# Two experts per gathered slot: value products on alternating 64-column halves of TensorE in a two-layer mixture kernel

## The chip, the cores and the metric

The kernel runs on one core of one Trainium2 chip. The metric is the device time in microseconds (us) of one execution. Each kernel is one launch. All data are float32. The core has TensorE (PE, whose weight loads are shown as PEld), VectorE (DVE), ScalarE (ACT), GpSimd (POOL) and SyncE (SP), and 16 DMA engines that bring data from the device memory (HBM) into on-chip memory (SBUF).

## The reference, cut to what matters

Two layers work on 256 latent tokens of 1024 channels (and in layer 0 also on 256 context tokens). Each layer mixes tokens and then applies an expert mixer, which takes most of the time:

```python
def peer(h, wq, subkeys, u_tab, v_tab):
    ...
    idx = i1 * PEER_KEYS + i2                 # 8 heads x 16 experts per token
    g = jax.nn.softmax(cv, axis=-1)
    ...
    def block(args):
        tb, ib, gb = args
        act = jax.nn.gelu(jnp.einsum('td,thkd->thk', tb, u_tab[ib]).astype(jnp.float32))
        return jnp.einsum('thk,thkd->td', (gb * act).astype(tb.dtype), v_tab[ib])
```

Each token picks 128 of 16384 experts. For each of them a row u (1024 numbers) is multiplied with the token's activations to one number, which goes through gelu and is weighted, and a row v (1024 numbers) is added to the token's output with that weight. The kernel does this for latent tokens of layer 0 (stage 0), context tokens of layer 0 (stage 1) and latent tokens of layer 1 (stage 2): 3 stages of two 128-token tiles with 128 experts each, 768 tile-experts of 1 MB, 805 MB in all.

## The kernel before

**The slot pipeline.** A slot `s` is one tile-expert: partition p of the ring buffer `uv` (RING = 8 places of 8 KB per partition) holds row u and row v of the expert that token p has in place `s % 128`. The work of a slot passes through all engines:

- POOL (`gathers`, L1050) waits until the ring place is free (`uv_used`) and issues an indirect DMA of 128 rows of 8 KB.
- DVE (`dot`, L1593) multiplies u with the token's activations `h2` and sums to `dots`.
- ACT (`weigh`, L1221, L1223, L1225) takes gelu, multiplies by the gate `gw`, and writes the diagonal matrix `diag` (128x128, weight of token p at row p, column p).
- PE (`add_values`, L983) multiplies `diag` (the stationary side) with v in two products of 512 columns and adds them up in PSUM, in `acc`. Each product in float32 is two MATMUL instructions in the profile. The last one frees the ring place.
- After the 128 slots of a tile DVE adds `acc`, times a gate, to `x` (`close`).

**The order of the work.** One list (`schedule`) is walked by PE, ACT and DVE. It has "slot" entries, "values" entries two slots later (LAG = 2), and between them "step" entries, which are all other work: projections (`query`, L786), scores (L957), searches for the best experts (`find`, six parts on DVE), the mixing of the next stage. `place` and `spread` fix the slot after which a step stands. Each engine works through its part strictly in order. Ahead of slot 0 (the opening, up to 176 us) and between the last slot of stage 1 and the first slot of stage 2 (the gap, about 1575 to 1664 us) only steps run, and there most ring places hold weight blocks. A gather into such a place waits until its block has been multiplied (`left`).

**What the change touches.** `turn_back` (L933) makes `h2`, token by token, out of `hT`, in which channels lie along the partitions: 8 transposes on PE and 2 evictions of 512 columns on ACT for each tile. It runs six times: for stage 0 tile 0 in the opening, stage 0 tile 1 soon after the first slots, twice among the slots for stage 1, for stage 2 tile 0 in the gap, and for stage 2 tile 1 some 60 us later. `find` part 5 (L1564, L1569) writes 16 expert numbers (`idx`) and 16 gates (`gw`) for each tile and head, 48 times in all.

## Time and profile before

| | before |
|---|---|
| median of 3 runs | 2360.29 us (2359.01 to 2362.58) |
| the profiled execution | span 2360.1 us, 0.2 us from the median |
| PE busy | 2079.7 us (88%) |
| DVE busy | 1609.6 us (68%) |
| POOL busy | 1019.5 us (43%) |
| ACT busy | 953.4 us (40%) |
| moved by DMA | 939.43 MB, 398 GB/s over the span |
| chain that ended last | PE 36%, DMA 33%, DVE 13% |

"Busy" of PE counts each matmul up to a modelled end, which overlaps the start of the next one, so it overstates how much of PE is used. "The chain that ended last" is followed backwards from the last instruction, each time to what released it. "GB/s" is what the 16 DMA engines moved in a stretch.

### The profile page before, as it was taken

What the parts mean: (1) busy time and instruction counts of PE and PEld (TensorE: products, weight loads), DVE (VectorE), ACT (ScalarE), POOL (GpSimd) and SP (SyncE); (2) the same over time, 40 slices, a digit from 0 to 9 for tenths busy, and PEclk for the clock granted to TensorE, in tenths of its full rate; (3) what the DMA queues carried; (4) which work ended last, traced back from release to release, by engine and by line L of the source; (5) the groups of instructions that cost most, each with busy time, mean ns of one, the idle gap of its engine ahead of it and who ended that gap; (6) DMA issues with size and microseconds to landing.
All of it is one profiled execution on the core that took longest, in us unless ns stands there. A gap on an engine that the chain in (4) does not pass through costs nothing.

```text
span 2360.1 us, 24134 instructions
## 1 busy us (share of the span) xinstructions
PE 2079.7 (88%) x6896; PEld 1123.8 (48%) x6896; DVE 1609.6 (68%) x3952; ACT 953.4 (40%) x2791; POOL 1019.5 (43%) x868
## 2 busy tenths in 40 slices
PE   8998998899998988988898998798899988777787
PEld 7775554455564434544454544346455533222222
DVE  3855668967766568788866677855765887666454
ACT  2014434543334444444454333534543444444333
POOL 0004444344334444444444454530333555566774
PEclk9999999999999999999999999999999999999999
DMA  9979999999999999999999999996799999999997
GB/s 400 375 291 382 395 399 421 407 421 421 421 420 421 415 421 404 421 421 417 391 421 421 421 421 421 416 370 254 284 365 379 415 421 421 422 421 421 422 421 318
DMA packets 132595, 939.43 MB, mean 398 GB/s; under 512 B 14720, under 2 KB 17920, under 8 KB 18944
## 3 DMA queue, kind: packets, MB, share of 16 engines
q0 software_dynamic: 110592, 805.36, 82.8%
q1 hardware_dynamic: 21888, 132.68, 13.8%
q8 instruction: 55, 0.90, 0.2%
q14 instruction: 60, 0.49, 0.1%
HBM read 936.93 MB, written 1.05 MB: 397 GB/s over the span
## 4 chain that ended last, share of the span: by engine, by line
PE 36%; DMA 33%; DVE 13%; issue 7%; POOL 6%; ACT 5%; POOLq 0%; SPq 0%; DVEq 0%; ACTq 0%
DMA uv<-uv_dram,stage_idx 31%; PE psum L983 19%; PE psum L786 9%; DVE uv L1593 6%; POOL uv L1050 5%; PE psum L768 4%; PE psum L926 1%; DMA uv<-in_dram 1%; ACT diag L1225 1%; DMA uv<-ada_dram 1%; ACT wv L1223 1%; DVE h L1282 1%; PE psum L704 1%; PE psum L957 1%; ACT gel L1221 1%
## 5 line engine op out<-in xcount | busy, mean ns | idle before, releaser
L983 PE MATMUL psum<-uv,diag 128*128 128x512 f32 x3072 | 1447.1, 611 | 227.8 <-ACT diag L1225 217.6
L1050 POOL DMA_INDIRECT uv<-uv_dram,stage_idx x768 | 985.9, 1284 | 1052.3 <-PE psum L983 829.5
L1593 DVE CUSTOM_DVE_ANT_0 uv<-uv,h 128x1024 f32<-128x1024 f32 x768 | 935.1, 1226 | 554.6 <-DMA uv<-uv_dram,stage_idx 545.2
L983 PEld LDWEIGHTS psum<-uv,diag 128*128 128x128 f32 x3072 | 562.1, 192 | 1006.5 <-issue 505.3
L1221 ACT ACTIVATE gel<-dots 128x1 f32<-128x1 f32 x768 | 155.3, 202 | 1060.6 <-DVE dots L1593 1059.7
L1225 ACT ACTIVATE diag<-const,wv 128x128 f32<-128x128 f32 x768 | 308.3, 401 | 25.0
L786 PE MATMUL psum<-hT,wring 128*128 128x256 f32 (+1 forms) x1312 | 273.0, 361 | 0.7 <-ACT hT L1091 0.7
L786 PEld LDWEIGHTS psum<-hT,wring 128*128 128x128 f32 x1312 | 233.1, 190 | 60.2 <-issue 33.0
L1223 ACT ACTIVATE wv<-gel,gw 128x1 f32<-128x1 f32 x768 | 226.3, 295 | 25.0
L1038 POOL COPY stage_idx<-idx 128x8 uint32 (+1 forms) x96 | 33.4, 348 | 265.4 <-DVE idx L1564 264.7
L1073 ACT ACTIVATE work<-psum 128x256 f32<-128x256 f32 (+2 forms) x123 | 47.7, 389 | 128.5 <-PE psum L786 102.1
L768 PE MATMUL psum<-wring,hT 128*128 128x256 f32 x320 | 72.7, 382 | 0.7 <-ACT hT L1091 0.7
L768 PEld LDWEIGHTS psum<-wring,hT 128*128 128x128 f32 x320 | 61.6, 193 | 17.3 <-issue 8.8
L1221 ACT ACT_TABLE_LOAD x50 | 64.2, 1283 | 0.9
L1593 DVE DVE_READ_ACCUMULATOR2_ANT dots<- 128x1 f32 x768 | 62.8, 82 | 0.0
L786 PE MATMUL psum<-hT,uv 128*128 128x256 f32 (+1 forms) x224 | 52.4, 395 | 5.4 <-DVE sp_t L1364 2.8
L1532 DVE MAX8 work<-work 128x8 f32<-128x128 f32 x80 | 17.9, 279 | 50.8 <-ACT work L1073 50.7
L1401 DVE SCALAR_TENSOR_TENSOR work<-work,const 128x256 f32<-128x256 f32 x120 | 50.1, 478 | 0.0
L786 PEld LDWEIGHTS psum<-hT,uv 128*128 128x128 f32 x224 | 43.6, 208 | 13.3 <-issue 5.7
L1192 ACT ACT_TABLE_LOAD x32 | 41.1, 1283 | 0.6
L957 PEld LDWEIGHTS psum<-keys,work 128*128 128x128 f32 x192 | 26.6, 197 | 18.2 <-issue 11.6
L1282 DVE CUSTOM_DVE_ANT_0 h<-uv,h 128x1024 f32<-128x1024 f32 x28 | 33.2, 1221 | 3.0 <-issue 2.3
(224 smaller groups left out, 1289.8 us busy)
## 6 DMA issues: line engine op xcount, KB each, us to landing
uv<-ada_dram SPq DMA_DIRECT2D x30, 1024.0 KB, 15.8
wring<-in_dram SPq DMA_DIRECT2D x25, 1024.0 KB, 9.5
wring<-wq_dram SPq DMA_DIRECT2D x24, 1024.0 KB, 11.2
uv<-uv_dram,stage_idx POOLq DMA_INDIRECT x768, 14.2
uv<-in_dram SPq DMA_DIRECT2D x9, 1024.0 KB, 13.5
uv<-ada_t_dram SPq DMA_DIRECT2D x7, 1024.0 KB, 22.7
wring<-ada_dram SPq DMA_DIRECT2D x6, 1024.0 KB, 11.2
wring<-ada_t_dram SPq DMA_DIRECT2D x5, 1024.0 KB, 20.7
```

The source lines that it names most:

```text
L768: last = mm(bank[:, 0:BLK], src[:, k, :], w[:, k, :], start=(k == 0), stop=(k == KC - 1))
L786: last = mm(bank[:, 0:len(tiles) * P], w[:, k, i * P:(i + 1) * P], hT[:, k, tokens], start=(k == 0), stop=(k == KC - 1))
L957: last = mm(bank[:, o:o + P], qh[:, h % 2, q, t * P:(t + 1) * P], keys[:, h % 2, q * PK:(q + 1) * PK], start=True, stop=True)
L983: last = mm(acc[:, b, :], diag[:, s % RING, :], uv[:, s % RING, D + 512 * b:D + 512 * (b + 1)], start=(c == 0), stop=(c == NSEL - 1))
L1050: nc.gpsimd.indirect_dma_start(out=uv[:, s, :], out_offset=None, in_=tables[stage // 2], in_offset=bass.IndirectOffsetOnAxis(ap=stage_idx[ ...
L1073: mine.emptied(f(dst, src, func, **kw))
L1221: f(gel[:, r:r + 1], dots[:, r:r + 1], ACT.Gelu_apprx_tanh).then_inc(gelu_ready, 1)
L1223: f(wv[:, r:r + 1], gel[:, r:r + 1], ACT.Copy, scale=gw[:, (T // TT) % 2, T % TT, c:c + 1]).then_inc(wv_ready, 1)
L1225: f(diag[:, r, :], C("ident"), ACT.Copy, scale=wv[:, r:r + 1]).then_inc(diag_ready, 1)
L1282: v.tensor_tensor_reduce(out=row_tmp[:, j, :], in0=w, in1=c_rows[:, j, :], scale=1.0, scalar=0.0, op0=ALU.mult, op1=ALU.add, accum_out=ada ...
L1401: ops = [v.scalar_tensor_tensor(out=ccT[:, j, :], in0=cpT[:, j, k:k + TOK], scalar=w[:, j, k:k + 1], in1=ccT[:, j, :], op0=ALU.mult, op1=A ...
L1593: v.tensor_tensor_reduce(out=uv[:, r, 0:D], in0=uv[:, r, 0:D], in1=h2[:, row_of[stage], t, :], scale=1.0, scalar=0.0, op0=ALU.mult, op1=AL ...
```

## The change

A slot still is a gather of 128 rows, but it now serves 64 tokens with two experts each: slot 2m+j holds, for the 64 tokens of half j of the tile, expert 2m on partitions 0 to 63 and expert 2m+1 on partitions 64 to 127. The number of slots, gathers, rows and bytes stays. What follows from it:

- `diag` is 128x64: two 64x64 diagonals on top of each other (`pair_ident` scaled), so that the product adds the two experts of a token. Its result goes to 64 partitions of `acc`, and even and odd slots alternate between the halves.
- `h2` holds each half of a tile twice, once on each half of the partitions. `turn_back` makes it by 32 ordinary products with 64-column weights in place of 8 transposes, and 4 evictions in place of 2.
- `find` part 5 writes `idx` and `gw` in four pieces of 64x8 each in place of one of 128x16.
- `h2` takes 16 KB more per partition; the DMA descriptor area of the gathers is set to 4 KB per partition, from the default of 16 KB.
- ACT's first instruction also waits for DVE to make `pair_ident`.

```diff
+HALVES = 2
+HT = P // HALVES
+SCRATCH = 4096
...
-        h2 = sb("h2", [P, 2, TT, D])
+        h2 = sb("h2", [P, 2, TT, HALVES, D])
...
-        diag = sb("diag", [P, RING, P])
+        diag = sb("diag", [P, RING, HT])
+        pair_ident = sb("pair_ident", [P, HT])
...
+        ALL_HALVES = [(k, j) for k in range(HALVES) for j in range(HALVES)]
+        def rows_of(half):
+            return slice(half * HT, (half + 1) * HT)
...
             def turn_back(stage, t):
                 wait_hT()
-                for half in range(2):
-                    bank = to_act.open(pe)
-                    for i in range(4):
-                        last = turn(bank[:, i * P:(i + 1) * P], hT[:, half * 4 + i, t * P:(t + 1) * P], ident)
-                    to_act.fill(last)
+                for j in range(HALVES):
+                    half_tile = slice(t * P + j * HT, t * P + (j + 1) * HT)
+                    for half in range(2):
+                        bank = to_act.open(pe)
+                        for i in range(4):
+                            for k in range(HALVES):
+                                last = mm(bank[rows_of(k), i * P:(i + 1) * P], hT[:, half * 4 + i, half_tile], ident, start=True, stop=True)
+                        to_act.fill(last)
...
+                j = c % HALVES
                 for b in range(2):
-                    last = mm(acc[:, b, :], diag[:, s % RING, :], uv[:, s % RING, D + 512 * b:D + 512 * (b + 1)],
-                              start=(c == 0), stop=(c == NSEL - 1))
+                    last = mm(acc[j * HT:(j + 1) * HT, b, :], diag[:, s % RING, :], uv[:, s % RING, D + 512 * b:D + 512 * (b + 1)],
+                              start=(c < HALVES), stop=(c >= NSEL - HALVES))
...
-                f(diag[:, r, :], C("ident"), ACT.Copy, scale=wv[:, r:r + 1]).then_inc(diag_ready, 1)
+                f(diag[:, r, :], pair_ident[:, :], ACT.Copy, scale=wv[:, r:r + 1]).then_inc(diag_ready, 1)
...
+            act.wait_ge(pairs_set, 1)
...
-                        v.scalar_tensor_tensor(out=idx[:, stage % 2, t, slots[i]], in0=w.side_no[:, a + i, :], scalar=float(PK),
-                                               in1=w.side_no[:, n_t + a + i, :], op0=ALU.mult, op1=ALU.add).then_inc(idx_ready[t], 1)
+                        pairs = idx[:, stage % 2, t, slots[i]].rearrange("p (m j) -> p m j", j=HALVES)
+                        first, second = (w.side_no[:, q * n_t + a + i, :].rearrange("p (m k) -> p m k", k=HALVES) for q in range(2))
+                        for k, j in ALL_HALVES:
+                            done = v.scalar_tensor_tensor(out=pairs[rows_of(k), :, j], in0=first[rows_of(j), :, k], scalar=float(PK),
+                                                          in1=second[rows_of(j), :, k], op0=ALU.mult, op1=ALU.add)
+                        done.then_inc(idx_ready[t], 1)
...
-    nc = bacc.Bacc("TRN2", target_bir_lowering=False, num_devices=1)
+    nc = bacc.Bacc("TRN2", target_bir_lowering=False, num_devices=1, dynamic_dma_scratch_size=SCRATCH)
```

The order of steps and slots does not move. What changes in it are the instructions themselves. These are PE's rows in the opening just ahead of the first gathers, before (L786 query, L957 score, L938 turn back; a count is of products):

```order
L786 MATMUL psum<-hT,wring 128x128 x16
L957 MATMUL psum<-keys,work 128x128 x2
L938 MATMUL psum<-const,hT 128x128 x8
L786 MATMUL psum<-hT,wring 128x128 x16
L957 MATMUL psum<-keys,work 128x128 x2
```

And the same place in the changed kernel, where line numbers have moved (L798 query, L972 score, L953 turn back):

```order
L798 MATMUL psum<-hT,wring 128x128 x16
L972 MATMUL psum<-keys,work 128x128 x2
L953 MATMUL psum<-const,hT 64x128 x32
L798 MATMUL psum<-hT,wring 128x128 x16
L972 MATMUL psum<-keys,work 128x128 x2
```

Eight transposes have become 32 products of 64 result rows. The second place is PE among the first slots of the changed kernel (L999 value products, two to a slot; L764 transposes of normed rows):

```order
L780 MATMUL psum<-uv,work 128x256 x32
L999 MATMUL psum<-uv,diag 64x512 x16
L764 MATMUL psum<-const,work 128x128 x8
L999 MATMUL psum<-uv,diag 64x512 x2
L953 MATMUL psum<-const,hT 64x128 x32
L999 MATMUL psum<-uv,diag 64x512 x2
L798 MATMUL psum<-hT,wring 128x128 x8
L999 MATMUL psum<-uv,diag 64x512 x2
```

Nothing stands elsewhere than before, but value products and turn backs are now 64 rows high, and the steps between them 128. The third place is DVE in the first `find` part 5, before (L1561 sums, L1564 `idx`, L1569 `gw`):

```order
L1561 TENSOR_REDUCE work<-h2 128x16 x2
L1564 SCALAR_TENSOR_TENSOR idx<-work 128x16
L1567 TENSOR_REDUCE work<-work 128x1
L1568 RECIPROCAL work<-work 128x1
L1569 TENSOR_SCALAR gw<-work 128x16
```

And in the changed kernel (L1585 `idx`, L1595 `gw`):

```order
L1579 TENSOR_REDUCE work<-h2 128x16 x2
L1585 SCALAR_TENSOR_TENSOR idx<-work 64x8 x4
L1589 TENSOR_REDUCE work<-work 128x1
L1590 RECIPROCAL work<-work 128x1
L1595 TENSOR_SCALAR gw<-work 64x8 x4
```

Three instructions more stand ahead of the signal for which POOL waits, and three more at the end.

## Rows read from the trace of the kernel before

**Rows 1.** The page: span; GB/s in 40 slices of 59 us; the gathers' queue.
```profile
span 2360.1 us, 24134 instructions
...
GB/s 400 375 291 382 395 399 421 407 421 421 421 420 421 415 421 404 421 421 417 391 421 421 421 421 421 416 370 254 284 365 379 415 421 421 422 421 421 422 421 318
...
q0 software_dynamic: 110592, 805.36, 82.8%
```

**Rows 2.** The page, groups: value products and their diagonals.
```profile
L983 PE MATMUL psum<-uv,diag 128*128 128x512 f32 x3072 | 1447.1, 611 | 227.8 <-ACT diag L1225 217.6
...
L1225 ACT ACTIVATE diag<-const,wv 128x128 f32<-128x128 f32 x768 | 308.3, 401 | 25.0
```

**Rows 3.** Timeline at 2200 us: start us, us, engine, line, operation.
```profile
2200.03 1.98 PE L983 MATMUL psum<-uv,diag 128*128 128x512 f32 x4 [0.51 <-ACT diag L1225]
...
2200.33 1.93 POOL L1050 DMA_INDIRECT uv<-uv_dram,stage_idx  x1 [0.53 <-issue]
...
2202.51 1.98 PE L983 MATMUL psum<-uv,diag 128*128 128x512 f32 x4 [0.50 <-ACT diag L1225]
```

**Rows 4.** Line 1050, us from issue to landing: at 2100 to 2300, at 1720 to 1740.
```profile
DMA to landing us min/median/max: 12.2/14.8/15.8
...
DMA to landing us min/median/max: 5.7/7.0/10.4
```

**Rows 5.** Windows of 10 us: busy us per engine, clock, DMA share, GB/s.
```profile
240.00:250.00 10.00, 9.39 (x22) 3.85 (x22) 9.65 (x33) 4.01 (x11) 6.48 (x7) 1.00 0.84 309
...
310.00:320.00 10.00, 10.00 (x37) 5.89 (x36) 7.30 (x24) 4.08 (x14) 4.34 (x4) 1.00 0.92 326
...
1560.00:1570.00 10.00, 10.00 (x25) 4.39 (x24) 6.50 (x11) 3.60 (x12) 4.65 (x4) 1.00 0.92 339
...
1740.00:1750.00 10.00, 10.00 (x32) 5.49 (x31) 5.30 (x19) 2.81 (x10) 2.60 (x4) 1.00 0.68 259
...
1810.00:1820.00 10.00, 10.00 (x32) 5.17 (x31) 2.31 (x3) 4.14 (x14) 4.15 (x5) 1.00 0.83 293
```

**Rows 6.** The chain, in time: start us, us, engine, tile, line.
```profile
218.10 0.87 PE psum L938 x8
218.97 1.72 PE psum L983 x4
220.69 1.78 PE psum L786 x16
...
316.71 5.15 PE psum L983 x12
...
1655.99 0.87 PE psum L938 x8
```

**Rows 7.** Timeline of PE: a turn back, a row-tiled and a column-tiled product.
```profile
55.76 2.75 PE L786 MATMUL psum<-hT,uv 128*128 128x256 f32 x12
...
58.44 1.93 PE L704 MATMUL psum<-uv,silu_c 128*32 128x256 f32 x32
...
1655.83 1.04 PE L938 MATMUL psum<-const,hT 128*128 128x128 f32 x8
...
1656.80 1.14 PE L862 MATMUL psum<-h 64*128 64x256 f32 x8
```

**Rows 8.** Timeline ahead of the first gathers.
```profile
170.85 0.71 PE L957 MATMUL psum<-keys,work 128*128 128x128 f32 x4 [1.00 <-ACT work L1073]
...
174.53 0.17 DVE L1564 SCALAR_TENSOR_TENSOR idx<-work 128x16 uint32<-128x16 f32 x1
...
174.62 0.16 DVE L1567 TENSOR_REDUCE work<-work 128x1 f32<-128x16 f32 x1
...
176.04 1.09 POOL L1050 DMA_INDIRECT uv<-uv_dram,stage_idx  x1 [0.97 <-PE psum L704]
```

**Rows 9.** Window of slots alone, and a group at the lower clock.
```profile
2100.00:2200.00 100.00, 76.96 (x158) 26.71 (x156) 61.35 (x143) 41.52 (x126) 64.39 (x44) 1.00 1.01 421
...
1964.30 5.41 PE psum L983 x8
```

More of the change, by code:

```diff
@@ L449, in build @@
         rr_root = rr_ms
-        h2_0 = h2[:, 0, :, :].rearrange("p a b -> p (a b)")
+        h2_0 = h2[:, 0, :, :, :].rearrange("p a j b -> p (a j b)")
         qT = view(h2_0, 0, HEADS, TOK)
@@ L467, in build @@
         vc_rows = [view(work, 5956, MIX), gate_peer[:, 0:MIX]]
-        kcT = h2[:, 1, 1, :].rearrange("p (a b) -> p a b", a=HEADS)
+        kcT = h2[:, 1, 1, 0, :].rearrange("p (a b) -> p a b", a=HEADS)
         orow = [slot(1, 0, MIX), gate_peer[:, MIX:]]
@@ L478, in build @@
         sc = view(work, 3072, 2, 2 * TT, PK)
-        h2_1 = h2[:, 1, :, :].rearrange("p a b -> p (a b)")
+        h2_1 = h2[:, 1, :, :, :].rearrange("p a j b -> p (a j b)")
         class Search:
@@ L506, in build @@
         row_of = (0, 1, 1)
-        c_rows = h2[:, 0, :, :]
-        row_tmp = h2[:, 1, :, :]
+        c_rows = h2[:, 0, 0, :, :]
+        row_tmp = h2[:, 1, 0, :, :]
         kept_sc = vx[:, :, :].rearrange("p a (b c) -> p (a b) c", c=2 * PK).rearrange("p h (q k) -> p h q k", q=2)
@@ L1167, in turn_back @@
             def turn_back(stage, t):
-                for half in range(2):
-                    empty(h2[:, row_of[stage], t, half * 512:(half + 1) * 512], 512)
+                for j in range(HALVES):
+                    for half in range(2):
+                        empty(h2[:, row_of[stage], t, j, half * 512:(half + 1) * 512], 512)
             def query(stage, h, q, tiles):
@@ L1568, in find @@
                     link(v.reciprocal(w.e_stat[:, 1, a:b], w.e_stat[:, 0, a:b]))
-                    weights = [v.tensor_scalar(gw[:, stage % 2, t, slots[i]], w.e16[:, a + i, :], w.e_stat[:, 1, a + i:a + i + 1], None,
-                                               ALU.mult) for i, t in enumerate(tiles)]
-                    link(*weights[:-1])
+                    for i, t in enumerate(tiles):
+                        pairs = gw[:, stage % 2, t, slots[i]].rearrange("p (m j) -> p m j", j=HALVES)
+                        terms = w.e16[:, a + i, :].rearrange("p (m k) -> p m k", k=HALVES)
+                        for half, j in ALL_HALVES:
+                            done = v.tensor_scalar(pairs[rows_of(half), :, j], terms[rows_of(j), :, half],
+                                                   w.e_stat[rows_of(j), 1, a + i:a + i + 1], None, ALU.mult)
                     if kept(stage, h, tiles):
-                        link(weights[-1])
+                        link(done)
                     else:
-                        weights[-1].then_inc(sc_used, 1)
+                        done.then_inc(sc_used, 1)
                         dve.wait_ge(sc_used, k)
@@ L1592, in dot @@
                 dve.wait_ge(uv_landed[r], 16 * (s // RING + 1))
-                v.tensor_tensor_reduce(out=uv[:, r, 0:D], in0=uv[:, r, 0:D], in1=h2[:, row_of[stage], t, :], scale=1.0, scalar=0.0,
+                v.tensor_tensor_reduce(out=uv[:, r, 0:D], in0=uv[:, r, 0:D], in1=h2[:, row_of[stage], t, s % HALVES, :], scale=1.0, scalar=0.0,
                                        op0=ALU.mult, op1=ALU.add, accum_out=dots[:, r:r + 1]).then_inc(dots_ready, 1)
@@ L1601, in close @@
                 dve.wait_ge(*taken["gate", stage, 1])
-                tmp = h2[:, row_of[stage], t, :]
+                tmp = h2[:, row_of[stage], t, 0, :]
                 v.tensor_tensor(tmp, acc.rearrange("p a b -> p (a b)"), gate_peer[:, :], ALU.mult).then_inc(acc_free, 1)
@@ L1614, in _ @@
             dve.wait_ge(const_loaded, 16)
+            v.tensor_tensor(pair_ident[:, :], C("ident")[:, 0:HT], C("ident")[:, HT:P], ALU.add).then_inc(pairs_set, 1)
             walk(steps, dot, nothing, close, takes)
```

2 lines of the change are left out of this document (1 added, 1 removed).

## The prediction, made before the changed kernel ran

> **What bounds the kernel now.** I read the page first, and in it the GB/s of the 40 slices [rows 1]. Most slices stand at 421 and none is above 422: there the gathers take all that the DMA engines move. A gather of 1.05 MB at 421 GB/s takes 2.49 us, and the timeline at 2200 us shows that pace: PE starts a slot's products every 2.48 us and is done in four steps of 0.43, 1.72 us [rows 3]. POOL, too, cycles in about 2.48, but it need not: its DMA instruction lasts 1.93 there and 1.09 for the first gather [rows 8], and gathers land 14.8 us after issue, so about six are queued [rows 4]. In such a stretch a faster PE is worth nothing.
>
> So the most that the change can win is the time in which the DMA does not run at 421. Slice by slice, (421 - v)/421 x 59 us sums to 129 us: 28 in the opening (first three slices), 50 in the three around the gap (27 to 29), 14 in the last one, and 37 spread over stretches with slots.
>
> Next I read windows of 10 us where the rate falls among slots [rows 5]. PE is busy for all or nearly all of each: 309 GB/s at 240 us, 326 at 310, 339 at 1560, 259 at 1740, 293 at 1810. At 1740 the gathers land 7.0 us after issue, not 14.8 [rows 4]: PE is behind, frees places late, and the DMA queue runs dry. The chain says the same: at 218 us a slot's products alternate with a turn back and a query, at 316 three slots stand together (x12) [rows 6]. In these stretches PE's length matters, up and down.
>
> **The change part by part.**
>
> *Value products, alone.* The same 512 columns pass, so a slot on its own still takes 1.72 us [rows 3]. In the 64-wide form it must also change the form of the array against the 128-wide steps around it. Such a change has a price in rows 7: 12 products' instructions of 256 columns at 0.215 (half of 0.43) would end 2.58 after 55.76, but the 32-column products start 2.68 after; the turn back (eight instructions, 0.87 by rows 6) is followed by the 64-row form after 0.97. Both leave 0.10. A group of slots between steps pays it twice, 0.2 us. The 3072 instructions [rows 2] are 768 slots of four; in the order of the whole program they stand in 168 such groups, 35 of them with one slot.
>
> *Value products, in pairs.* Neighbouring slots now use different column halves. No row has 64-column halves. The nearest are the four 32-column quarters at 58.44: 32 instructions in 1.93, of which 0.38 is the recorded length of the last (as 11 x 0.215 + 0.38 = 2.75 for the 12 before), where one after another would take 32 x 0.215 = 6.9, so four run at once; and the 64-row halves at 1656.80, whose order is four instructions on one half and then four on the other, as with two slots: 1.14 in place of 1.9, so two at once [rows 7]. I take full overlap: a pair that stands ready takes 1.72, not 3.43. From below the saving is 0 (no overlap). It counts only where PE is behind.
>
> The Trainium skill (TensorE: Matmul & The Clock Gate, Part 3, The mechanism) says that matmuls start and end strictly in program order. By that, of four instructions on one half and four on the other only the last and first could overlap, and a pair would save 0.43 us and not 1.7. The row at 1656.80 speaks against it.
>
> *Turn backs.* 32 products are 64 instructions of 128 columns, 0.107 each: 6.9 us one after another, 3.6 with two halves at once (the inner loop alternates them), against 0.87. So +2.7 (bound +6.0), and 0.2 for the change of form where 128-wide work stands on both sides. Four of the six stand where PE is the chain [rows 6] or ahead of it:
> - Opening: +2.9. Behind it PE waited 1.00 for ACT, which absorbs that much; the first gather waited for PE's L704 (0.97) [rows 8]. Net +2.0. The first `idx` comes 3 x 0.09 later (0.09 is the distance from L1564 to the next), but it was ready 1.5 us ahead of the gather: nothing.
> - At 218: +2.7, and five single groups until 240 add 1.0. Gathers were still queued, so I let a third be absorbed: +2.5.
> - In the gap at 1656, with the attention behind it on PE: +2.9.
> - Near 1722: +2.7 and five single groups, +3.7; the DMA is dry there, all of it counts.
> - Stage 1's two are among slots at 421 GB/s: 0.
>
> *What pairs give back* in the dry windows: 310 us has 2.3 us of missing DMA (326 against 421), of which half, -1.2; slice 27 (around 1560, groups of two and three slots) misses 7.1, part of it the end of the gathers, so less than half, -3.3; 1810 (groups of two and three) misses 3.0, of which -2.0; slices 8 to 26 miss 11 us in all, where PE is full after a tile's close, -4.0.
>
> *DVE.* 6 instructions more in each of 48 finds, at 0.09: 26 us on an engine that is 68% busy, mostly beside the DMA. At 240 us, where DVE has 9.65 of 10 [rows 5], it lies on the path: +1.0 in all.
>
> *ACT.* `diag` shrinks from 128 to 64 columns, below 0.401 each [rows 2], and turn backs add 12 evictions. ACT waits in every slot; 0. The wait for `pair_ident` (one small DVE instruction) lies behind the first weights: 0 to 0.3, taken 0.
>
> *Descriptor area.* A gather is 144 packets (110592/768), nine per DMA engine [rows 1], and about six are in flight [rows 4]: 54 per engine. No row shows how much of the area that fills. If POOL were held up by it, a delay up to 0.8 per gather would hide (1.93 against 1.09). I take 0; the other end is a gather issued only when the one before has landed, 5.7 us at least [rows 4].
>
> The Trainium skill (DMA: Bandwidth & Descriptors, Terms) gives 16 bytes for a descriptor. An estimate from that page: 4096/16 = 256 places per engine against 54, so no wait, the value that I take anyway.
>
> *Sum:* 2.0 + 2.5 + 2.9 + 3.7 - 1.2 - 3.3 - 2.0 - 4.0 + 1.0 = +1.6 us. The profiled span is 0.2 below the median, so the time is 2362 us: no change, as a measurement tells one from 0.2% (4.7 us) on. The gain goes nowhere because it falls where the DMA is the bound; losses and gains at the edges nearly cancel.
>
> **The rivals.**
>
> *Faster: PE's catching up is worth more* (0.26). If pairs recover half of the 37 us missing among slots (19) and the costs above (about 12) stay, the time is 2353. For it: PE is full in each dry window. Against it: the driest one, 1740, follows single slots between steps, which gain nothing. It decides once pairs recover more than 17 us.
>
> *Slower: halves overlap little* (0.14). By the program-order rule above, give-backs of 10.5 shrink to 2.6 and the group of six slots before 250 us helps less (+1.5): +11, 2371. With no overlap at all turn backs cost 6.0 each and nothing comes back: +25, 2385. Against: rows 7.
>
> *Slower: the clock* (0.09). Where slots stand alone, PE is idle for 0.77 of 2.49 us and the granted clock is 1.00, the 2.4 GHz level [rows 9]. A half-wide product may count for less. At the lower level eight instructions took 5.41 [rows 9] in place of 3.43. If halves overlap, PE keeps up even at 3.4 per slot; stretches at PE's limit lose 2 us per fall, and ten more falls make 2380. Without overlap 185 last slots at 3.4 in place of 2.49 give over 2500.
>
> *Slower: gathers held up by the smaller area* (0.04), 2400 and more. It decides when POOL's instruction grows by more than 0.8.
>
> *Slower, turn backs and switches dearer than taken* (0.05): 2368.
>
> **How the numbers follow.** No change has 0.42, faster 0.26, slower 0.14 + 0.09 + 0.04 + 0.05 = 0.32. The likeliest case by itself spans 2356 to 2367. The range that leaves out no more than 2 in 10 reaches down to the middle of the faster case, 2352, and up to 2382, past the overlap cases and most of the clock's.
>
> **What would show it.** In the changed profile: value products still 0.43 apart within a slot, and two slots' products starting side by side where PE is behind; L953 x64 in 3.6 us (6.9 if halves do not overlap); 421 GB/s in the same slices; first gather near 178 us, stage 2's first gather near 1661 (1664 before); fewer missing GB/s at 1560 and 1810, more at 1740; POOL's instruction at 1 to 1.93 as before; a granted clock of 1.00 in the last 300 us. Wrong would make it: a lower clock in slot-only stretches, a landing time that shrinks while POOL waits for itself, or an opening that moves by more than 5 us.

## The result and the profile after

The kernel after takes **2378.77 us** (median of 6 runs, 2373.55 to 2382.47), the kernel before 2361.43 on the same chip (6 runs, 2359.01 to 2364.91). The ratio is 1.0074, 95% interval 1.0062 to 1.0085: 17 us slower. The time lies in the range that was given, but not in the likeliest case.

First the page of the kernel after: the span, the GB/s of 40 slices (59.5 us each) and the gathers' queue, as in [rows 1]; then groups as in [rows 2], and from the part on the chain its shares by engine.

```profile
span 2380.2 us, 25105 instructions
...
GB/s 402 369 286 367 366 399 420 391 422 421 421 420 421 420 420 403 417 421 394 416 421 421 421 421 421 417 373 227 297 343 350 421 417 420 422 421 422 421 421 317
...
q0 software_dynamic: 110592, 805.36, 82.4%
...
DMA 40%; PE 29%; DVE 19%; issue 5%; ACT 5%; POOL 1%; POOLq 0%; SPq 0%; DVEq 0%; ACTq 0%
...
L999 PE MATMUL psum<-uv,diag 128*64 128x512 f32 x3072 | 1264.9, 630 | 363.9 <-ACT diag L1242 353.2
L1066 POOL DMA_INDIRECT uv<-uv_dram,stage_idx x768 | 898.3, 1170 | 1151.7 <-PE psum L999 939.3
...
L1242 ACT ACTIVATE diag<-pair_ident,wv 128x64 f32<-128x64 f32 x768 | 267.1, 348 | 25.0
```

The value products are busy for 1265 us where they were for 1447 [rows 2], and the DMA still runs at 421 in most slices. So 182 us of value products are gone (TensorE as a whole is busy for 1961.1 us and not 2079.7) and the kernel is slower: the loss is in the slices that were below 421 before. The fourth and fifth slice show 367 and 366 where [rows 1] has 382 and 395; slices 30 and 31 show 343 and 350 where it has 365 and 379. Missing GB/s at 59 us a slice make about 6 us in the first place and 7 in the second. Around the gap, slices 28 and 29 show 227 and 297 where [rows 1] has 254 and 284, 2 us more.

Windows of the same two kernels by stage say it again. These are of the kernel after (columns as in [rows 5]: busy us of PE, PEld, DVE, ACT and POOL, clock, DMA share, GB/s):

```profile
180.00:330.00 150.00, 133.34 (x551) 74.31 (x550) 90.01 (x246) 58.96 (x176) 53.17 (x53) 0.97 0.94 371
330.00:1550.00 1220.00, 1015.55 (x3306) 444.96 (x3305) 932.74 (x2369) 501.78 (x1542) 553.45 (x506) 0.96 1.01 417
1660.00:1870.00 210.00, 183.31 (x873) 99.44 (x872) 141.30 (x415) 91.52 (x257) 70.90 (x70) 0.95 0.85 332
```

The same windows of the kernel before:

```profile
180.00:330.00 150.00, 137.81 (x503) 86.58 (x502) 90.68 (x244) 60.78 (x179) 60.07 (x54) 0.98 0.97 388
330.00:1550.00 1220.00, 1102.43 (x3199) 584.68 (x3198) 896.28 (x2194) 526.59 (x1547) 569.38 (x507) 0.99 1.01 417
1660.00:1870.00 210.00, 191.78 (x729) 114.67 (x729) 144.35 (x403) 96.80 (x271) 81.36 (x79) 0.98 0.92 369
```

In the long middle both have 417: 87 us less of TensorE won nothing. Most of the loss comes from the openings of stages 0 and 2, where 388 becomes 371 and 369 becomes 332. The starts of VectorE's dots, compared one by one, say where in time: in the two profiled executions, which are 20 us apart, the kernel after is 8 us behind at 338 us (times of the kernel before), 10 at the end of stage 1, 12 behind the gap, 13 at 1726 and 19 at 1762, and 20 from 1980 on.

What TensorE does there is in the chain of the kernel after (start, us, engine, tile, line; L953 is the turn back, L798 a projection, L972 the scores of a query), to be read beside [rows 6]:

```profile
165.40 3.64 PE psum L953 x64
...
228.05 1.86 PE psum L999 x4
229.91 2.00 PE psum L798 x16
...
232.97 1.86 PE psum L999 x4
234.83 3.65 PE psum L798 x16
238.49 1.86 PE psum L999 x4
```

The chain of the kernel before at the same work (L983 the slot, L786 the two-tile projection):

```profile
227.06 1.72 PE psum L983 x4
228.78 3.45 PE psum L786 x16
232.23 1.72 PE psum L983 x4
```

Read the lengths: a single slot takes 1.86 and not 1.72 [rows 6], the single-tile step behind it 2.00 and not 1.78, and the two-tile step 3.65 where the kernel before has 3.45. One change of form and back costs 0.14 + 0.20 = **0.34 us**, not the 0.2 that I worked with. The turn back takes 3.64, as predicted.

Further on in the same chain stand pairs:

```profile
310.44 3.65 PE psum L798 x16
314.09 1.87 PE psum L999 x8
315.96 3.65 PE psum L798 x16
...
1833.34 3.58 PE psum L999 x12
```

Two slots in 1.87 where one took 1.72 [rows 6]: the halves overlap in full. By the trace the starts of these eight instructions lie in four pairs 0.43 apart, the second slot's first instruction 0.01 behind the first slot's first. The Trainium skill (TensorE: Matmul & The Clock Gate, Part 3, The mechanism) has matmuls start and end strictly in program order; here the second slot's four come behind the first slot's four in the program and run beside them, so this trace contradicts it.

### The profile page after: what moved, and what is told of

Read it like the earlier page. It is cut to its first block, busy times and chain, and to the rows that moved or that the text cites. A ratio compares the mean times of both kernels' runs of the same rounds, so it can differ in the third digit from the quotient of the medians.

```text
span 2380.2 us, 25105 instructions
## 1 busy us (share of the span) xinstructions
PE 1961.1 (82%) x7232; PEld 908.7 (38%) x7232; DVE 1676.6 (70%) x4241; ACT 919.4 (39%) x2803; POOL 935.9 (39%) x868
## 3 DMA queue, kind: packets, MB, share of 16 engines
q1 hardware_dynamic: 21888, 132.68, 13.7%
## 4 chain that ended last, share of the span: by engine, by line
DMA 40%; PE 29%; DVE 19%; issue 5%; ACT 5%; POOL 1%; POOLq 0%; SPq 0%; DVEq 0%; ACTq 0%
DMA uv<-uv_dram,stage_idx 38%; PE psum L999 13%; PE psum L798 8%; DVE uv L1618 8%; PE psum L780 3%; ACT diag L1242 1%; DMA uv<-in_dram 1%; ACT wv L1240 1%; DVE gw L1595 1%; POOL uv L1066 1%; DMA uv<-ada_dram 1%; PE psum L953 1%; PE psum L938 1%; PE psum L716 1%; DVE h L1300 1%
## 5 line engine op out<-in xcount | busy, mean ns | idle before, releaser
L999 PE MATMUL psum<-uv,diag 128*64 128x512 f32 x3072 | 1264.9, 630 | 363.9 <-ACT diag L1242 353.2
L1066 POOL DMA_INDIRECT uv<-uv_dram,stage_idx x768 | 898.3, 1170 | 1151.7 <-PE psum L999 939.3
L999 PEld LDWEIGHTS psum<-uv,diag 128*64 128x64 f32 x3072 | 340.3, 141 | 1180.5 <-ACT diag L1242 704.2
L798 PE MATMUL psum<-hT,wring 128*128 128x256 f32 (+1 forms) x1312 | 281.4, 368 | 0.7 <-ACT hT L1107 0.7
L1242 ACT ACTIVATE diag<-pair_ident,wv 128x64 f32<-128x64 f32 x768 | 267.1, 348 | 25.0
L798 PEld LDWEIGHTS psum<-hT,wring 128*128 128x128 f32 x1312 | 227.9, 191 | 86.8 <-issue 53.9
L780 PEld LDWEIGHTS psum<-wring,hT 128*128 128x128 f32 x320 | 59.4, 190 | 22.0 <-issue 13.7
L798 PE MATMUL psum<-hT,uv 128*128 128x256 f32 (+1 forms) x224 | 52.1, 393 | 5.2 <-DVE sp_t L1382 2.8
L798 PEld LDWEIGHTS psum<-hT,uv 128*128 128x128 f32 x224 | 43.4, 207 | 13.0 <-issue 3.6
L1595 DVE TENSOR_SCALAR gw<-work 64x8 f32<-64x8 f32 x176 | 45.2, 257 | 3.2
```

The costliest lines, as they stand in the source:

```text
L780: last = mm(bank[:, 0:BLK], src[:, k, :], w[:, k, :], start=(k == 0), stop=(k == KC - 1))
L798: last = mm(bank[:, 0:len(tiles) * P], w[:, k, i * P:(i + 1) * P], hT[:, k, tokens], start=(k == 0), stop=(k == KC - 1))
L999: last = mm(acc[j * HT:(j + 1) * HT, b, :], diag[:, s % RING, :], uv[:, s % RING, D + 512 * b:D + 512 * (b + 1)], start=(c < HALVES), stop ...
L1066: nc.gpsimd.indirect_dma_start(out=uv[:, s, :], out_offset=None, in_=tables[stage // 2], in_offset=bass.IndirectOffsetOnAxis(ap=stage_idx[ ...
L1242: f(diag[:, r, :], pair_ident[:, :], ACT.Copy, scale=wv[:, r:r + 1]).then_inc(diag_ready, 1)
L1595: done = v.tensor_scalar(pairs[rows_of(half), :, j], terms[rows_of(j), :, half], w.e_stat[rows_of(j), 1, a + i:a + i + 1], None, ALU.mult)
```

## The experiments

Four explanations stood at the start. **T1**: the time is lost on TensorE, by turn backs and changes of form where TensorE is the bound. **T2**: it is VectorE, whose busy time grew from 1609.6 to 1676.6 us. **T3**: the granted clock, which stood at 1.2 GHz in 39 stretches of 171.5 us in all, in 21 of 93.2 us before. **T4**: the descriptor area. The first four kernels are the kernel before with one piece of the change each. The runs below were made on four chips, each with runs of the kernel before beside it. Kernels are therefore compared by their ratios, of which 0.001 is 2.4 us, and not by their times.

**The area alone** (`num_devices=1, dynamic_dma_scratch_size=4096` in the kernel before).

> The kernel before with the descriptor area of 4 KB and nothing else. Theory T1 (the time is lost in work ahead of the stretches where the gathers are not the bound: the 32 products of a turn back and the switches of form of the value products) and theory T2 (it is VectorE's idx and gw in pieces of 64 partitions, 67 us of busy time more) both expect no change here: 2361.4 us, within 0.1%. Theory T4 (the smaller area makes GpSimd wait when it issues gathers) expects most of the +17.3 us: over 2370 us, with the indirect issues of GpSimd clearly above their mean of 1284 ns.

2360.93 us, ratio 1.0000, interval 0.9989 to 1.0011. In the page the DMA instruction of POOL lasts as long as before (mean 1282 ns, where it was 1284):

```profile
L1050 POOL DMA_INDIRECT uv<-uv_dram,stage_idx x768 | 984.9, 1282 | 1054.9 <-PE psum L983 786.2
```

T4 is out.

**The pieces of VectorE alone.**

```diff
-                    weights = [v.tensor_scalar(gw[:, stage % 2, t, slots[i]], w.e16[:, a + i, :], w.e_stat[:, 1, a + i:a + i + 1], None,
-                                               ALU.mult) for i, t in enumerate(tiles)]
+                        halves = gw[:, stage % 2, t, slots[i]].rearrange("p (m j) -> p m j", j=2)
+                        terms = w.e16[:, a + i, :].rearrange("p (m k) -> p m k", k=2)
+                        for r in (slice(0, 64), slice(64, P)):
+                            for j in range(2):
+                                done = v.tensor_scalar(halves[r, :, j], terms[r, :, j], w.e_stat[r, 1, a + i:a + i + 1], None, ALU.mult)
```

(and `idx` in the same way)

> The kernel before with idx and gw each written in four pieces of 64 partitions by 8, without crossing the halves (the values are the same as before; 1,152 instructions more on VectorE as in the kernel after). Theory T2: VectorE's 64 us more of busy time stand on the chain at the openings of the tiles and the result is +8 to +15 us (2370 to 2376). Theory T1: VectorE has slack almost everywhere, +0 to +4 us (2361 to 2365). If the pieces cost 163 and 257 ns as in the kernel after, VectorE's busy time becomes about 1674 us; if it is the crossing of partitions that is dear, it stays nearer 1635.

2361.61 us, ratio 1.0000, 0.9988 to 1.0011, with the engine's busy time up by 46. Groups of this kernel:

```profile
L1579 DVE TENSOR_SCALAR gw<-work 64x8 f32<-64x8 f32 x176 | 33.4, 238 | 1.9
L1568 DVE SCALAR_TENSOR_TENSOR idx<-work 64x8 uint32<-64x8 f32 x176 | 21.3, 160 | 2.1
```

By themselves the pieces are hidden. A piece of 64x8 costs as much as the whole 128x16 did, which took 239 and 172 ns. The crossing adds little to an instruction: the pieces of the kernel after, with crossing, take 257 and 163 ns.

**The turn back alone.** h2 gets the kernel after's second copy, and:

```diff
-                for half in range(2):
-                    bank = to_act.open(pe)
-                    for i in range(4):
-                        last = turn(bank[:, i * P:(i + 1) * P], hT[:, half * 4 + i, t * P:(t + 1) * P], ident)
-                    to_act.fill(last)
+                for _ in range(2):
+                    for half in range(2):
+                        bank = to_act.open(pe)
+                        for i in range(4):
+                            for k in range(2):
+                                last = mm(bank[64 * k:64 * k + 64, i * P:(i + 1) * P],
+                                          hT[:, half * 4 + i, t * P + 64 * k:t * P + 64 * k + 64], ident, start=True, stop=True)
+                        to_act.fill(last)
```

> The kernel before with the turn back of the kernel after alone: 32 products with 64 rows out and four evictions for a tile, which write the tile twice (both copies are the whole tile in order, so the result is as before; the descriptor area is 3 KB to make room). Each turn back should take 3.64 us of TensorE rather than 0.87. Theory T1: the turn backs that come before a dry stretch (opening, 218, gap, 1722) lose 2 to 2.8 us each for good, +6 to +11 us in all (2367 to 2372). Theory T2: the turn backs are worth little, +0 to +4 us. Theory T3 (the granted clock falls more often because the value products of a pair are short): no share of it here, the low clock stays near 93 us.

2373.44 us, ratio 1.0049, 1.0034 to 1.0064: 11.6 us. Dot by dot against the kernel before, the two profiles part by 1.0 us ahead of the first dot, by 3.4 between the dots at 184 and 249 us, by 4.4 over the gap (dots 508 to 512) and by 2.7 between 1729 and 1753: 11.5 in all, at the places named in the prediction. The timeline of the last one:

```profile
1731.85 3.71 PE L940 MATMUL psum<-const,hT 128*64 128x128 f32 x64 [0.72 <-ACT hT L1094]
```

**The change of form alone.**

```diff
-                    last = mm(acc[:, b, :], diag[:, s % RING, :], uv[:, s % RING, D + 512 * b:D + 512 * (b + 1)],
-                              start=(c == 0), stop=(c == NSEL - 1))
+                    for j in range(2):
+                        last = mm(acc[64 * j:64 * j + 64, b, :], diag[:, s % RING, 64 * j:64 * j + 64],
+                                  uv[:, s % RING, D + 512 * b:D + 512 * (b + 1)], start=(c == 0), stop=(c == NSEL - 1))
```

> The kernel before with every slot's two value products cut into four of 64 columns each in turn (left half, right half), so that the form of the products switches as often as in the kernel after, but slots are not paired and nothing else is changed. With 0.34 us for the two switches around a group of slots (1.86 for a single slot as against 1.72, and 3.65 as against 3.45 for the step behind it) theory T1 expects +3 to +7 us from the some 20 groups in the two stretches where TensorE is the bound (2364 to 2368), and nothing in the stretches where the gathers are. Theory T3: if narrow products lower the granted clock, it falls here too, more than 21 times and for more than 93 us, and the time rises by the share of the +17 us that is due to it. Theory T2: no change.

2373.23 us, ratio 1.0052, 1.0033 to 1.0071: 12.3 us, above the 3 to 7 that I expected of T1. The granted clock fell 16 times for 63.9 us, less than before, so narrow products alone don't make it fall more often. The timeline of this kernel at a change:

```profile
298.79 1.94 PE L984 MATMUL psum<-uv,diag 128*64 128x512 f32 x8
300.66 0.60 PE L957 MATMUL psum<-keys,work 128*128 128x128 f32 x3
```

The eight instructions take 1.87 from the first start to the next line's first, for one slot, as in the kernel after for two. The starts behind these rows show where the 0.34 lies: the last projection's start stands 0.31 ahead of the first narrow one (0.22 elsewhere), the first narrow pair lasts 0.47 and the last 0.52 (0.43 between), and the first instruction of the step behind it 0.21 here (0.11 elsewhere; 0.32 and 0.22 where that step is a two-tile projection). Why 12 and not 7: every group pays, not the single ones alone. Of the 168 groups 23 begin between 180 and 330 us and 31 between 1660 and 1900; 54 x 0.34 = 18.4 is the most that it can cost there, and two thirds of that arrive. That every group pays is argued from the lengths in the trace; no run changed the single groups alone.

**Both together, still without pairs.**

> The kernel before with both of the edits that cost time by themselves: the turn back of 32 products with four evictions (alone 2373.44 us, ratio 1.0049) and every slot's value products in column halves (alone 2373.23 us, 1.0052). Slots are not paired, idx and gw stay whole. Theory T1 (both are time of TensorE ahead of stretches that the gathers don't bound, and the time is kept to the end): the two add, +22 to +24 us, 2383 to 2386 us, and then the pairing of slots in the kernel after (2378.77) gives back 5 to 7 us. Theory T5 (the two hide each other, pairs give back nothing): 2377 to 2380 us, as the kernel after.

2382.32 us, ratio 1.0090, 1.0074 to 1.0107: 21.3 us. The two nearly add, and by the medians the kernel is slower than the kernel after (1.0074), though the two intervals meet. So the rest of the change gives something back. Its granted clock fell only 17 times, for 63.4 us, and it is the slowest of all kernels: a loss of this size comes about without T3.

The other kernels are the kernel after with one thing undone. **Wide value products:**

```diff
-                    last = mm(acc[j * HT:(j + 1) * HT, b, :], diag[:, s % RING, :], uv[:, s % RING, D + 512 * b:D + 512 * (b + 1)],
-                              start=(c < HALVES), stop=(c >= NSEL - HALVES))
+                    last = mm(acc[:, b, :], diag[:, s % RING, :], uv[:, s % RING, D + 512 * b:D + 512 * (b + 1)],
+                              start=(c == 0), stop=(c == NSEL - 1))
...
-                f(diag[:, r, :], pair_ident[:, :], ACT.Copy, scale=wv[:, r:r + 1]).then_inc(diag_ready, 1)
+                f(diag[:, r, c % HALVES * HT:(c % HALVES + 1) * HT], pair_ident[:, :], ACT.Copy, scale=wv[:, r:r + 1]).then_inc(diag_ready, 1)
```

> The kernel after with value products of 128 columns (each slot's diag is 128x128 with its other half zero, zeroed once; descriptor area 3 KB to make room; the output is the same). Nothing switches form and the products of two slots no longer overlap; the turn back and the pieces of idx and gw stay. Theory T1: it loses both the switches (about 12 us by the kernel with forms alone) and the overlap of pairs (5 to 7 us of gain), so it comes to the time of the turn back alone, 2372 to 2375 us. Theory T5 (pairs give back nothing): 2366 to 2368, which is after minus the 12 us of the forms. Theory T3 (the granted clock): it falls 39 times in the kernel after and 21 before; here it should fall some 20 times again, and what T3 would claim of the time lies in the stretch 330 to 1560 us.

2373.95 us, ratio 1.0047, 1.0031 to 1.0064: the time of the turn back alone, as T1 has it, and not the 2366 to 2368 of T5. Changes of form and pairs' overlap leave together, and the pieces of VectorE show no cost here, within some 5 us to either side.

**A short turn back that keeps both copies:**

```diff
-                for j in range(HALVES):
...
-                                last = mm(bank[rows_of(k), i * P:(i + 1) * P], hT[:, half * 4 + i, half_tile], ident, start=True, stop=True)
+                for half in range(2):
+                    bank = to_act.open(pe)
+                    for i in range(4):
+                        last = turn(bank[:, i * P:(i + 1) * P], hT[:, half * 4 + i, t * P:(t + 1) * P], ident)
+                    to_act.fill(last)
...
+                    bank = mine.full_bank(act)
+                    for k, j in ALL_HALVES:
+                        last = f(h2[rows_of(k), row_of[stage], t, j, half * 512:(half + 1) * 512], bank[rows_of(j), 0:512], ACT.Copy)
+                    mine.emptied(last)
```

> The kernel after with another turn back (the output is the same): 8 turns of the whole tile into two banks, as before, and ScalarE copies each bank in four pieces of 64 partitions, crossing the halves, so that both copies of h2 come out as in the kernel after. TensorE should take 0.87 us for a turn back rather than 3.64, ScalarE some 8 pieces of 0.4 to 0.6 us rather than four of that length. Theory T1: the turn backs' 12 us go, or the most of them, if ScalarE's pieces are hidden: 2366 to 2370 us. Theory T6 (what counts in the turn back is the later landing of h2, since the first dot of a tile waits for its last eviction): ScalarE's chain is longer than in the kernel after, and the time stays 2375 us or more.

2371.47 us, ratio 1.0032, 1.0018 to 1.0045: by the ratios about 10 of the turn backs' 12 us come back. The timeline at the opening:

```profile
165.25 1.04 PE L950 MATMUL psum<-const,hT 128*128 128x128 f32 x8
...
165.89 4.83 ACT L1184 ACTIVATE h<-psum 64x512 f32<-64x512 f32 x8
```

ScalarE's eight copies end at 170.7, later than the four evictions of the kernel after (169.7), and it gains all the same: T6 fails, TensorE's time is what counts. The granted clock fell 52 times for 213.6 us in this kernel, more than in any other, and it is faster than the kernel after; that is the second fact against T3.

**Whole idx and gw in the kernel after.** This leaves out the crossing of the halves, so other rows are gathered.

```diff
-                        for half, j in ALL_HALVES:
-                            done = v.tensor_scalar(pairs[rows_of(half), :, j], terms[rows_of(j), :, half],
-                                                   w.e_stat[rows_of(j), 1, a + i:a + i + 1], None, ALU.mult)
+                        done = v.tensor_scalar(pairs, terms, w.e_stat[:, 1, a + i:a + i + 1], None, ALU.mult)
```

> The kernel after with idx and gw written in one piece over 128 partitions, with the same slots' order; left out is the crossing of the two partition halves, so the slots gather other rows and the output is another. VectorE's busy time should fall from 1677 to about 1635 us or less. Theory T1: nothing changes, 2377 to 2380 us (the pieces alone in the kernel before cost 0.2 us). Theory T2 (in the kernel after the openings are later, and there the pieces stand on the chain, as the chain's rows of gw suggest): 2368 to 2374 us.

2372.81 us, ratio 1.0043, 1.0027 to 1.0058, inside the range that T2 gave: by the ratios 7 us less than the kernel after, some 5 to either side, though the same pieces cost nothing in the kernel before. The run changes more than the pieces, though. Other rows are gathered, and the granted clock is higher in every one of its runs (0.971 to 0.976 over the span, 0.962 to 0.968 in the kernel after). The chain of the kernel after has the pieces of `gw` in this place:

```profile
1868.37 0.20 DVE work L1589
1868.79 0.43 DVE gw L1595
1869.23 0.23 DVE gw L1595
1869.48 0.23 DVE gw L1595
```

**No wide products, no long turn back.** Both edits in the kernel after; what stays is the pairing, VectorE's pieces and ScalarE's copies.

> The kernel after with the turn back of 8 whole turns (ScalarE crosses the halves, as in the run that gave a ratio of 1.0032) and with value products of 128 columns (as in the run that gave 1.0047): of the change only the pairing of experts in a slot, the pieces of idx and gw, ScalarE's extra copies and the descriptor area stay. The output is the same. Theory T1 (turn backs and forms are the whole loss, pairs the only gain): 2360 to 2364 us, no change. Theory T2 (the pieces on VectorE cost 4 to 7 us in the kernel after, as the run with whole idx and gw suggests, 1.0043 as against 1.0074): 2366 to 2370 us.

2365.23 us, ratio 1.0019, 1.0009 to 1.0028: 4.5 us over the kernel before. The time lies between the two expectations. The two TensorE edits carry most of the 17 us; a rest of 4 or 5 stays with what this kernel keeps, above all VectorE's and ScalarE's added work, which this run doesn't part.

**Narrow projections.** If a change of form is what costs, the steps beside the slots can take the slots' form. On top of the short turn back:

```diff
                 for k in range(KC):
-                    last = mm(bank[:, 0:len(tiles) * P], w[:, k, i * P:(i + 1) * P], hT[:, k, tokens],
-                              start=(k == 0), stop=(k == KC - 1))
+                    if len(tiles) > 1:
+                        for j in range(HALVES):
+                            last = mm(bank[rows_of(j), 0:len(tiles) * P], w[:, k, i * P + j * HT:i * P + (j + 1) * HT], hT[:, k, tokens],
+                                      start=(k == 0), stop=(k == KC - 1))
```

(and the token-major products of 256 columns likewise)

> The kernel after with the turn back of 8 whole turns and with the projections beside the slots in the slots' form: each product with 128 columns of weights and 256 moving columns is cut into two of 64 columns, one for each half (the output is the same). If the switch of form costs 0.34 us because a product that spans both halves waits until both are drained, no switch is left between these steps and the value products, and the pairs' overlap of about 10 us stays: theory T1 expects 2357 to 2363 us, 8 to 14 less than the 2371.47 of the kernel with the turn back alone mended, and a step of 8 such products at 3.45 us or little more. Theory T7 (two halves with 256 moving columns don't run side by side as those with 512 do, as the turn back's with 128 don't: 3.64 us for 64 instructions): a step of 8 products takes up to 3.64 us or more, the openings grow, and the time is 2375 us or more.

2363.59 us, ratio 1.0011, 1.0002 to 1.0020: by the ratios 5 us less than with the short turn back alone (1.0032), less than the 8 to 14 that T1 expected. The last step was to take the single-tile projections and the scores into halves as well.

> The kernel before this one (narrow projections, 2363.59 us, ratio 1.0011) with the steps of 128 moving columns in halves too: the projections of a single tile and the scores of the queries, each product of 128 columns of weights cut into two of 64. The output is the same. Theory T1: the switches around these steps go (some 18 of them in the two stretches where TensorE is the bound, 0.34 us each, of which about half reached the end so far): 2358 to 2361 us, level with the kernel before or a little under it. Theory T7 (at 128 moving columns the halves don't run side by side, so that 64 instructions of a turn back took 3.64 us): a single-tile step grows from 1.78 us to 3.5, a scores step from 0.87 to 1.7, and the time is 2370 us or more.

**2355.82 us, ratio 0.9973, 0.9961 to 0.9984**: faster than both kernels, by 6.3 us against the one before and by 9 against the kernel of the last run. T7 fails, and its premise was a misreading: 64 instructions of a turn back at 0.107 each would take 6.9 one after another, so at 3.64 they already ran two at once. Its chain at the same place as above (L800 is the projection, L972 the scores):

```profile
299.90 3.24 PE psum L800 x29
303.14 1.77 PE psum L999 x8
304.91 3.40 PE psum L800 x30
308.31 1.67 PE psum L999 x8
309.97 1.03 PE psum L972 x14
```

Two slots and a projection take 304.91 - 299.90 = 5.01 us, where the kernel after needs 1.87 + 3.65 = 5.52. The first slot product starts 0.16 ahead of the projection's last instruction, as its timeline shows:

```profile
302.81 0.59 PE L999 MATMUL psum<-uv,diag 128*64 128x512 f32 x1
302.97 0.38 PE L800 MATMUL psum<-hT,wring 128*64 128x256 f32 x1
303.19 1.08 PE L999 MATMUL psum<-uv,diag 128*64 128x512 f32 x4
```

That is one reason why it gained more than T1 expected. The other is that a slot on its own, which uses one half of the columns, now runs beside the narrow products of the step behind it, on the half that it leaves free. The timeline of a slot and its two-tile step:

```profile
232.51 0.59 PE L999 MATMUL psum<-uv,diag 128*64 128x512 f32 x1
232.66 0.59 PE L800 MATMUL psum<-hT,wring 128*64 128x256 f32 x2
232.94 0.59 PE L999 MATMUL psum<-uv,diag 128*64 128x512 f32 x1
233.10 0.38 PE L800 MATMUL psum<-hT,wring 128*64 128x256 f32 x1
233.37 0.59 PE L999 MATMUL psum<-uv,diag 128*64 128x512 f32 x1
233.37 0.65 PE L800 MATMUL psum<-hT,wring 128*64 128x256 f32 x2
233.79 0.59 PE L999 MATMUL psum<-uv,diag 128*64 128x512 f32 x1
234.22 3.40 PE L800 MATMUL psum<-hT,wring 128*64 128x256 f32 x29
237.30 0.59 PE L999 MATMUL psum<-uv,diag 128*64 128x512 f32 x1
```

From one slot to the next it is 4.79 us. The kernel after needs 1.86 + 3.65 = 5.51 for the same work and the kernel before 1.72 + 3.45 = 5.17. So the 14 us between this kernel and the one with the short turn back alone are not all changes of form: some of them are this overlap, and no run parts the two.

The windows of this kernel, to be set beside those of the first section:

```profile
180.00:330.00 150.00, 128.46 (x833) 68.62 (x830) 97.70 (x272) 64.23 (x191) 59.42 (x58) 0.98 0.98 402
...
1660.00:1870.00 210.00, 179.02 (x1037) 93.24 (x1034) 155.35 (x445) 99.38 (x285) 80.68 (x83) 0.93 0.96 383
```

402 and 383 GB/s, above the 388 and 369 of the kernel before.

**The same with whole idx and gw**, the crossing left out as above:

> The same kernel with idx and gw written in one piece over 128 partitions; left out is the crossing of the two partition halves, so that the slots gather other rows and the output is another. Theory T2 (what is left over of the change is VectorE's pieces, 64 us more of busy time, worth 3 to 7 us): 2354 to 2358 us, clearly under the kernel before. Theory T1 alone (the pieces are hidden, as they were in the kernel before): the same time as the kernel beside it, within 0.1%.

2352.86 us, ratio 0.9959, 0.9944 to 0.9974. It is 3 us under its neighbour, which ran on the same chip: its slowest of 7 runs took 2355.30, and 7 of the neighbour's 12 took longer. So there is a difference, of 1 to 6 us by the spread of the runs, and that is what T2 expected. But here too the rows gathered are others and the granted clock is higher in every run (0.968 to 0.973, the neighbour's 0.958 to 0.966), so this doesn't settle how much of it is VectorE's pieces.

## Why the prediction was right or wrong, point by point

The time lay in the range, and the likeliest case (2362, no change) did not come. That the range reached so far is luck: it went up to 2382 for halves that overlap little and for the clock, and the halves overlapped in full. Ratios times 2361 give the terms as measured: turn backs +11.6, changes of form +12.3, the two together +21.3; from there to the kernel after with whole idx and gw -11.1 (the pairs); and from there to the kernel after +7.3 (the pieces). The last two are differences between runs with intervals of their own, and good to some 5 us to either side.

- **"There the gathers take all that the DMA engines move."** Right. The middle kept its 417 GB/s with 87 us less of TensorE.
- **Changes of form, "A group of slots between steps pays it twice, 0.2 us", counted for ten single groups: +2.0. This is the step that failed.** The price was 0.34, since neither row behind it ([rows 7]) held both ends of a group; and the groups of two and three slots pay it as well. In the two stretches where TensorE is the bound there are 54 groups and not ten. The term measured 12.3, interval 8 to 17.
- **Turn backs, +9.1 of the sum** (opening 2.0, 218 with 1.5 of its 2.5, gap 2.9, 1722 with 2.7). Measured 11.6, interval 8 to 15, with each turn back of the length forecast, 3.64. Right in sum, within what was measured; by place the opening took 1.0 and not 2.0, the one at 218 3.4, the gap 4.4, and the one near 1722 2.7. So by these profiles nothing of the one at 218 was absorbed.
- **"What pairs give back", -10.5 in four places.** The size was right, -11.1 by the runs with the two edits of TensorE in place. The places were right but for one. Dot by dot, the kernel after with whole idx and gw gains on the one with both TensorE edits and no pairs 3.1 us between 312 and 344 us (forecast 1.2), 3.7 at the end of stage 1, between 1562 and 1592 (forecast 3.3 for slice 27), and 3.8 between 1681 and 1881 (forecast 2.0), of which 1.2 are lost again by 1995. In the middle, from 344 to 1562 us, the distance between the two ends as it began, to 0.2 us, after going up to 1.8 each way: the 4.0 forecast there did not come. Another 1.2 are lost over the gap. These are single executions. The rival *faster* needed pairs worth over 17 us.
- **"I take full overlap."** Right: x8 in 1.87.
- **VectorE, +26 us busy and +1.0 on the path.** Wrong in the first number: +67, since I priced an added instruction by the distance of 0.09 between two starts, where each of the 64-partition pieces lasts 163 and 257 ns. What it costs in time is not settled. It was 0 in the kernel before (interval 2.6 us to either side), about 7 in the kernel after, 0 in the kernel after with wide products, and 3 in the fastest one. The 7 and the 3 come from kernels that also gather other rows and have a higher granted clock in every run, a rival that no run takes out; by the bound of the next point but one it is worth 3 us at most in the stretches where TensorE is the bound. It may also depend on whether a find ends late at that place; no run shows the mechanism.
- **The descriptor area, ACT's `diag`, the wait for `pair_ident`: 0.** The area measured 0.
- **The rival of the clock.** The falls came (39 and not 21). From 1909 us on TensorE has nothing but slots; six of the falls lie between there and 2064 us (five in the kernel before), none from there to 2378, and the DMA ran at 419 GB/s from 1920 to 2070. The slowest kernel fell 17 times and the fastest one with the right rows 44 times, so the falls don't go with the time. That no microsecond of the 17 is theirs is not shown, but the rows bound it: in the windows 180 to 330 and 1660 to 1870, where TensorE is the bound, the lower level held for 30.7 us in the kernel after and for 17.0 before. At half the clock 13.7 us more are worth 7 us of TensorE's work at most. The kernel with whole idx and gw has 23.9 us there, which is worth 3 us at most against the kernel after.
- **The rival *turn backs and switches dearer than taken*, 0.05 and 2368.** This is the one that came, and both its chance and its price were too small.

## What to carry to other kernels

Count a change of TensorE's tile form as an expense of its own, 0.34 us for going and coming back here, and count it at every place where wide and narrow products meet while TensorE is the bound. If one kind of product becomes narrow, make its neighbours narrow too: cut into two column halves they take no longer, their tails overlap, and a slot on one half runs beside them on the other. And before a saving on an engine is booked, split its time by stage: value products that were busy for 182 us less were worth about 11 us of time, and those came where TensorE was the bound, at the openings and at the end of stage 1.

## What the runs showed of the hardware that was not expected

- A change of form waits for what is under way: the last narrow products lasted 0.52 in place of 0.43 until the next line began, and with one form only, a slot's first product started 0.16 ahead of the projection's last instruction. The Trainium skill (TensorEngine Tiling (Array Packing), Key Properties) says that changing the tiling mode drains the engine; the trace agrees (with a change of form, the first narrow product starts 0.31 behind the start of the step's last instruction, where 0.22 is the usual distance), and adds the price of 0.34 for both directions.
- Products with 64 weight columns and 256 or 128 moving columns run side by side as those with 512 do: the 64 instructions of a turn back in 3.64 us, and a projection's 32 instructions in pairs 0.22 apart, as the 16 wide ones.
- A slot's products on one column half and a projection's on the other run at the same time: one slot and a two-tile step in 4.79 us, in 5.17 with wide products.
- An instruction of VectorE on 64x8 values costs as much as on 128x16: 238 ns against 239 (`gw`), 160 against 172 (`idx`); with crossing of the halves 257 and 163.
- ScalarE's copies from 64 partitions to the other 64, 64x512, took 592 ns each, as those of 128x512 (594).
- Falls of TensorE's granted clock cost nothing that shows where the DMA is the bound: from 330 to 1550 us the lower level held for 88.7 us in the kernel after and for 30.7 in the kernel before, and both moved 417 GB/s. The falls were 16 to 21 in the kernels without pairs and 39 to 52 in those with paired narrow products and the right rows (27 and 33 with whole idx and gw, 25 and 29 with pairs and wide products). TensorE's busy time alone doesn't order them: 33 falls at 1912 us busy, 27 at 1966, 39 at 1961.
